# Recurrent scores built in seven halving levels, and prompt attention on queries reversed within each tile

## The reference, cut to what matters

```
# recurrence, per head: S_t = diag(f_t) S_{t-1} + k_t v_t^T ; o_t = S_t^T q_t, written in chunks
decay = exp(where(causal, G[t] - G[s], NEG))          # G: running sum of log f, per channel d
attn  = einsum("bhtd,bhtsd,bhsd->bhts", q, decay, k)  # scores inside a chunk
o     = attn @ v + einsum("bhtd,bhdv->bhtv", q * exp(G), S)
S     = exp(g_end) * S + einsum("bhsd,bhsv->bhdv", k * exp(g_end - G), v)

# prompt attention: three parts with one relative bias by distance, then a gated sum
s = einsum("btgrd,bngd->bgrtn", q, k) + rel_bias[bucket(t - n)]   # selected, window, compressed keys
p = softmax(where(valid, s, NEG)) ; o = p @ v
o_c = g[0] * o_cmp + g[1] * o_sel + g[2] * o_win
```

## Time and profile before

| what | us |
|---|---|
| median of 3 runs (3782.72 to 3790.37) | 3783.14 |
| the profiled execution, its time | 3777.45 |
| its span, first to last instruction | 3775.9 |
| recurrence, 429.2 to 1092.7 | 663.5 |
| attention rows, 1092.7 to 1171.5 | 78.8 |
| prompt attention, 1908.6 to 2346.0 | 437.4 |
| trunk, from 2657.1 | 1118.8 |

### The profile page before, as it was taken

How to read it: one execution, slowest core, us unless ns; L and a number is a source line. 1 busy time by engine, 2 the same in 40 slices (tenths; PEclk the granted TensorE clock), 3 DMA queues, 4 the chain that set the end, 5 groups by cost and what they waited for, 6 DMA issues and landing times. The chain is left out here.

```text
span 3775.9 us, 50148 instructions
## 1 busy us (share of the span) xinstructions
PE 3189.6 (84%) x19173; PEld 2945.0 (78%) x19173; DVE 1425.3 (38%) x3099; ACT 816.0 (22%) x1469; POOL 336.7 (9%) x484
## 2 busy tenths in 40 slices
PE   7999799999942788888569997447799799999999
PEld 6999798998941677677457776334699699999999
DVE  4122234234243454555335554862444422112221
ACT  3100101011000333333134454100322222111110
POOL 0011111111101222221000000000000200000000
PEclk9999878788865899999678999556899899999999
DMA  3222202112136554443121111102533111221122
GB/s 127 86 83 79 80 31 88 63 60 88 35 121 209 133 135 118 115 127 97 36 71 40 40 40 37 11 5 71 188 110 122 40 44 44 91 92 40 44 83 90
DMA packets 123489, 303.51 MB, mean 80 GB/s; under 512 B 36434, under 2 KB 60721, under 8 KB 121889
## 3 DMA queue, kind: packets, MB, share of 16 engines
q1 hardware_dynamic: 96250, 232.21, 20.6%
q0 software_dynamic: 15776, 56.93, 3.9%
q10 hardware_dynamic: 11280, 11.89, 1.0%
HBM read 233.49 MB, written 71.03 MB: 81 GB/s over the span
## 5 line engine op out<-in xcount | busy, mean ns | idle before, releaser
L2252 PE MATMUL tr_ps<-tr_act_in_r,tr_w_hi 128*128 128x364 f32 (+1 forms) x2496 | 487.3, 331 | 0.0
L2252 PEld LDWEIGHTS tr_ps<-tr_act_in_r,tr_w_hi 128*128 128x128 f32 x2496 | 428.8, 190 | 0.0
L2252 PE MATMUL tr_ps<-tr_wide_r,tr_w_hi 128*128 128x364 f32 (+1 forms) x1632 | 317.7, 330 | 0.0
L2252 PE MATMUL tr_ps<-tr_act_in_r,tr_w_r 128*128 128x364 f32 (+1 forms) x1248 | 278.8, 332 | 29.9 <-POOL tr_act_in_r L2233 22.5
L2252 PEld LDWEIGHTS tr_ps<-tr_wide_r,tr_w_hi 128*128 128x128 f32 x1632 | 279.2, 189 | 0.0
L54 PE MATMUL hg_ps<-tokens_hi,hg_gw_r 128*128 128x364 f32 (+1 forms) x576 | 224.3, 389 | 28.7 <-POOL hg_gw_r L1472 19.8
L2252 PEld LDWEIGHTS tr_ps<-tr_act_in_r,tr_w_r 128*128 128x128 f32 x1248 | 218.3, 190 | 32.9 <-issue 24.7
L2403 DVE TENSOR_TENSOR tr_w_r<-tr_w,tr_w_hi 128x1024 fp32r<-128x1024 f32 (+2 forms) x76 | 103.7, 1365 | 338.8 <-ACT tr_w_hi L2325 338.8
L55 PE MATMUL hg_ps<-tokens_r,hg_gw_hi 128*128 128x364 f32 (+1 forms) x576 | 217.9, 378 | 0.0
L56 PE MATMUL hg_ps<-tokens_hi,hg_gw_hi 128*128 128x364 f32 (+1 forms) x576 | 216.3, 376 | 0.0
L2252 PE MATMUL tr_ps<-tr_wide_r,tr_w_r 128*128 128x364 f32 (+1 forms) x816 | 181.1, 330 | 10.9 <-DVE tr_w_r L2403 10.9
(11 more groups left out here) (541 smaller groups left out, 6116.7 us busy)
## 6 DMA issues: line engine op xcount, KB each, us to landing
sa_pages<-cache_in SPq DMA_DIRECT2D x256, 256.0 KB, 3.9
tr_w<-w_gate_up_in SPq DMA_DIRECT2D x44, 512.0 KB, 3.6
proj_feat<-hg_g_stage POOLq DMA_DIRECT2D x24, 544.0 KB
tr_act_in<-proj_feat SPq DMA_DIRECT2D x24, 544.0 KB, 5.1
hg_gw<-w_gates_in SPq DMA_DIRECT2D x24, 512.0 KB
tr_w<-w_down_in SPq DMA_DIRECT2D x16, 704.0 KB, 4.1
np_wt<-w_tok_in SPq DMA_DIRECT2D x6, 1552.0 KB, 7.1
proj_tok<-np_stage_t POOLq DMA_DIRECT2D x48, 194.0 KB, 2.2
```

Of the source, the lines that this page charges most:

```text
L2252: last = pe.matmul(ps[:, 3 * bs + c, 0:z - a], wp, xp[:, k, a:z], start=(k == 0 and n == 0), stop=(k == len(tiles) - 1 and n == 2))
```

## The change

**Recurrence.** The two loops over `j` and `i` give way to seven levels `l` = 0..6. Within a tile, pairs of neighbouring halves of width 2^l meet: the queries of the later half (64 columns of each tile) are multiplied by all 128 keys, and a mask `pair` keeps the products of the earlier half of the same pair. After a level VectorE multiplies the earlier half's keys, and the later half's queries, by the other half's total decay, in place, so that keys are decayed to the end of a block twice as wide and queries to its beginning. The plain product of keys and queries (`diag_mm`) gives the diagonal. TensorE does the diagonal and each level for 8 prompt tiles, and for the sample tile in levels 0 to 2 only. Gate pieces are distributed anew: one behind the diagonal, one behind each level, and one (index 16) behind the outputs, ahead of the sum of squares. The sample's scores are multiplied by its values in one product instead of eight. The clearing of `kb` and `kt` goes; a 229 KB constant `pair` takes the place of a 64 KB one.

**Attention.** Prompt queries are reversed within each tile by a product with `flip` instead of a transpose; the bias table is then used as the DMA writes it, in two buffers, and the products and copies at each head's start go. The branch gates are turned by one product at the stage's start, ahead of their exponential, and the trunk turns the output rows back by a product with `flip`.

```
 # attention_rows_stage
+            sp.dma_start(flip[:], flip_in).then_inc(const_in, 16)
-                    pe.transpose(ps[...], rows[0:tn, t % 2, slot:slot + 2]..., ident[0:tn, 0:tn]).then_inc(tr_done, 1)
+                    if n < 4 and t0 < TP:
+                        pe.matmul(dst, src, flip[:], start=True, stop=True).then_inc(tr_done, 1)
+                    else:
+                        pe.transpose(dst, src, ident[0:tn, 0:tn]).then_inc(tr_done, 1)
 # prompt_attention_stage
+            pe.matmul(ps[:, 7, 0:NT * 3 * NH], flip[:], gates_in[:]..., start=True, stop=True).then_inc(S["gates_mm"], 1)
             for h in range(NH):
                 pe.wait_ge(head_in[h % 2], 64 * (h // 2 + 1))
-                for n in range(NTB):
-                    a, z = n * BANK, min((n + 1) * BANK, TW)
-                    if h >= 1:
-                        pe.wait_ge(S["sel_neg"], NT * h)
-                        pe.wait_ge(S["win_neg"], NT * h)
-                    pe.matmul(ps[:, n, 0:z - a], flip[:], strip[:, h % 2, a:z], start=True, stop=True)
-                pe.matmul(ps[:, NTB - 1, FAR:FAR + P], flip[:], strip_w[:, h % 2], start=True, stop=True).then_inc(S["flip_mm"], 1)
-                pe.wait_ge(S["table_set"], h + 1)
 # VectorE, per head
-                dve.wait_ge(S["flip_mm"], h + 1)
-                for n in range(NTB):
-                    a, z = n * BANK, min((n + 1) * BANK, TW)
-                    dve.tensor_copy(table[:, a:z], ps[:, n, 0:z - a])
-                dve.tensor_copy(far_w[:], ps[:, NTB - 1, FAR:FAR + P])
-                dve.drain().then_inc(S["table_set"], 1)
 # hgrn_stage, TensorE (the loops over j and i go)
+                pe.wait_ge(S["kq_set"], h + 1)
+                for t, (t0, tn) in enumerate(TILES):
+                    last = pe.matmul(ps[...], k[:, t0:t0 + tn], q[:, t0:t0 + tn], start=True, stop=True)
+                last.then_inc(S["diag_mm"], 1)
+                gate_pieces(h, AT_START, AT_START + 1)
+                for l in range(NLEV):
+                    pe.wait_ge(S["level_set"], h * (NLEV + 1) + (l + 1))
+                    if l >= 2:
+                        pe.wait_ge(S["scores_taken"], h * (NLEV + 1) + l)
+                    for t, (t0, tn) in enumerate(TILES):
...
+                        last = pe.matmul(dst..., k[:, t0:t0 + tn], halves(q_dec[:, t0:t0 + tn], l)[:, :, 1], start=True, stop=True)
+                    last.then_inc(S["level_mm"], 1)
+                    if l + 1 < NLEV:
+                        gate_pieces(h, AT_START + l + 1, AT_START + l + 2)
+                gate_pieces(h, AT_START + NLEV, AT_START + NLEV + 1)
...
                 last.then_inc(S["o_mm"], 1)
+                gate_pieces(h, AT_START + 11, 3 * CHUNKS - 1)
                 pe.wait_ge(S["sq_done"], h * 3 + 3)
                 pe.wait_ge(S["o_copied"], h + 2)
 # hgrn_stage, VectorE, per head (the memsets and both loops go)
+                dve.tensor_tensor(q_dec[:], q[:], f[:], ALU.mult).then_inc(S["level_set"], 1)
...
+                for l in range(NLEV):
+                    dve.wait_ge(S["level_mm"], h * NLEV + (l + 1))
+                    end = T if l < SLEV else TP
+                    late = halves(totals[l][:, 0:end >> l], 0)[:, :, :, 0]
+                    dve.tensor_tensor(totals[l + 1][:], late[:, :, 0], late[:, :, 1], ALU.mult)
+                    for x, t in ((0, k), (1, q_dec)):
+                        half = halves(t[:, 0:end], l)[:, :, x]
+                        dve.tensor_tensor(half, half, late[:, :, 1 - x:2 - x].to_broadcast(...), ALU.mult)
+                    dve.drain().then_inc(S["level_set"], 1)
+                    met = part[:, l % 2]
+                    dve.tensor_tensor(met, ps[:, 2 + l % 2, :]..., pair[:, l:l + 1].to_broadcast(...), ALU.mult).then_inc(S["scores_taken"], 1)
+                    dve.drain()
+                    a = halves(attn[:, 0:NTL]..., l)[:, :, 1]
+                    dve.tensor_tensor(a, a, met..., ALU.add)
 # trunk_stage
-                    last = pe.transpose(ps[...], rows[:, t, k * P:(k + 1) * P], ident[:])
+                    last = pe.matmul(ps[...], rows[:, t, k * P:(k + 1) * P], flip[:], start=True, stop=True)
```

More of the change, by code:

```diff
@@ L1387, in hgrn_stage @@
         sig = sb("sig", [P, 2, T])
-        decay = sb("decay", [P, T])
         q_dec = sb("q_dec", [P, T])
-        q_tile = sb("q_tile", [P, TP])
-        before = sb("before", [P, NTL, NBK + 1])
-        kb = sb("kb", [P, 2, T])
-        kt = sb("kt", [P, 2, TP])
+        totals = [f] + [sb(f"total{l}", [P, (T if l <= SLEV else TP) >> l]) for l in range(1, NLEV + 1)]
+        part = sb("part", [P, 2, NTL, HALF])
+        part_s = ctx.enter_context(nc.sbuf_tensor("hg_part_s", [SB * ST, SLEV, SB * ST // 2], F32))
         attn = sb("attn", [P, NTL + 1, P])
@@ L1563, in _ @@
-                for i in range(1, NBK):
-                    pe.wait_ge(S["kt_set"], h * NBK + i)
-                    for t in range(NTL):
-                        last = pe.matmul(ps[:, 3 + t // 4, (t % 4) * P + i * HC:(t % 4) * P + (i + 1) * HC], kt[:, i % 2, t * P:(t + 1) * P],
-                                         q_dec[:, t * P + i * HC:t * P + (i + 1) * HC], start=True, stop=True)
-                    last.then_inc(S["off_mm"], 1)
-                    if i % 3 == 0:
-                        gate_pieces(h, AT_START + 3 + i // 3, AT_START + 4 + i // 3)
@@ new lines, in _ @@
+                gate_pieces(h, AT_START + NLEV, AT_START + NLEV + 1)
+                pe.wait_ge(S["level_set"], h * (NLEV + 1) + (NLEV + 1))
+                for t in range(NTL):
+                    last = pe.transpose(ps[:, t // 4, (t % 4) * P:(t % 4 + 1) * P], k[:, t * P:(t + 1) * P], ident[:])
+                    if t % 4 == 3:
+                        last.then_inc(S["tr"], 1)
+                pe.transpose(ps[0:SROWS, 4, 0:P], k[:, TP:T], ident[:]).then_inc(S["tr"], 1)
+                gate_pieces(h, AT_START + 8, AT_START + 9)
@@ L1605, in _ @@
                 for n, (a, z) in enumerate(COLS):
-                    last = pe.matmul(ps[:, (3, 4, 2)[n], 0:z - a], ones[:], rstd[:, a:z], start=True, stop=True)
+                    last = pe.matmul(ps[:, 2 + n, 0:z - a], ones[:], rstd[:, a:z], start=True, stop=True)
                 last.then_inc(S["ssq_mm"], 1)
@@ L1626, in _ @@
             dve.drain()
-            f8, k8, q8, d8, qd8 = blocks(f[:]), blocks(k[:]), blocks(q[:]), blocks(decay[:]), blocks(q_dec[:])
             with dve.Fori(0, NHG) as h:
@@ L1674, in _ @@
-                dve.tensor_tensor(attn[0:SB * ST, NTL, 0:SB * ST], ps[0:SB * ST, 2, 0:SB * ST], diag[0:SB * ST, 0:SB * ST], ALU.mult)
-                dve.drain()
-                for n in range(2):
-                    a = attn[:, 4 * n:4 * n + 4, HC:P]
-                    dve.tensor_tensor(a, a, ps[:, 3 + n, :].rearrange("p (t s) -> p t s", s=P)[:, :, HC:P], ALU.add)
-                dve.memset(states[:, 0], 0.0)
+                    last = dve.tensor_tensor(attn[:, 4 * n:4 * n + 4], ps[:, n, :].rearrange("p (t s) -> p t s", s=P), ident[:].unsqueeze(1).to_broadcast([P, 4, P]), ALU.mult)
@@ L2259, in _ @@
                 for k in range(4):
-                    last = pe.transpose(ps[:, 6 + t % 2, k * P:(k + 1) * P], rows[:, t, k * P:(k + 1) * P], ident[:])
+                    last = pe.matmul(ps[:, 6 + t % 2, k * P:(k + 1) * P], rows[:, t, k * P:(k + 1) * P], flip[:], start=True, stop=True)
                 last.then_inc(tr, 1)
@@ L2577, in shape_constants @@
     p = np.arange(P)
+    pair = np.stack([((p[:, None] >> l + 1 == q >> l + 1) & (p[:, None] >> l & 1 == 0)).astype(f4) for l in range(NLEV) for q in [p[(p >> l & 1) == 1]]], axis=1)
     return {
```

187 lines of the change are left out of this document (81 added, 106 removed).

## The result

The changed kernel takes 3503.4 us in the median of 4 runs (3486.0 to 3508.2); the kernel before, timed beside it, took 3782.9. The ratio is 0.9238, with an interval from 0.9207 to 0.9269.

What follows compares the result with a forecast made beforehand. TensorE's instructions and clock were taken to bound the recurrence; in prompt attention, engines took turns at head starts. Recurrence -195, prompt attention -60, attention rows +7.5, trunk +4 sum to -243.5 us: forecast 3538 us, range 3500 to 3570.

Steps and rivals of the forecast that it cites:

- the clock gave back: Recurrence: less time at 1.2 GHz behind sparse groups, 17.5 us a head gained; rival of levels keeping low clock, chance 0.13.
- 28, 3 and 3: Recurrence, us saved a head: 28 from 248 fewer instructions, 3 from the sample's outputs, 3 from the wait ahead of line 1606.
- the hold of VectorE: Recurrence levels: GpSimd holds VectorE 2.4 us against 1.8 spare; 2.5 us a head lost, between 0 and 10.
- 3.5 us of low clock: Recurrence, loss expected to stay a head: 1.8 us behind the sample outputs and as much at the loop's end.
- The cover: Recurrence: the gate piece behind each level hides VectorE's 2.2 us update; without it, 7 x 4 x 2.2 = 62 us.
- half as long and four times as dense: Recurrence: a level, 2.0 us of 64 columns, compared with a step of line 1557; no clock loss expected behind levels.
- The seven boundaries: Prompt attention: 6.37 us from first product to first score goes at seven head starts, 44.6 us saved.
- The first scores: Prompt attention's start: scores wait for split queries and begin at 1936.2 in place of 1941.10, 4.9 us earlier.
- the clock term: Prompt attention: faster clock returns between nothing and 57 us; 10 taken.
- Neither rival: Prompt attention: all low-clock stretches go, 57 us back, 3491 (chance 0.07); or 1.2 GHz at every head's start, 3578 (0.05).
- Attention rows, +8.3 for +7.5: Attention rows: four more instructions a tile, 0.9 us each of eight tiles, plus 0.4 for one more DMA: +7.5 us.
- The step that failed: Trunk: two tiles need about 3.5 us of TensorE against a 2.53 period, so TensorE sets it: +4 us, between 0 and 6.

Runs made afterwards that it cites:

- the square: Changed kernel and three variants: levels 2 to 6 at 8 columns, 3502.7 us; all levels' products issued twice, 3551.5 us; levels 2 to 6 with both, 3561.6 us.
- the filling: Changed kernel plus one unread 320-column product behind the transposes of the first two tiles of prompt attention's heads 1 to 7 (also "the filled starts"): 3479.8 us.

## Why the prediction was right, and where its terms were off

**Recurrence, -224 for -195.** The mechanism held: TensorE set the pace with its instructions and its clock. The terms that were off, in a middle head's 55.4 us against 49: the clock gave back about 21.4 in place of 17.5 (what is left of 55.4 less 28, 3 and 3), and the hold of VectorE cost 0 in place of 2.5. Most of this clock can be seen on instructions that did not change. The gate products are the same 1,728 in both kernels; a third of them, before (after, they stand above):

```profile
L54 PE MATMUL hg_ps<-tokens_hi,hg_gw_r 128*128 128x364 f32 (+1 forms) x576 | 224.3, 389 | 28.7 <-POOL hg_gw_r L1472 19.8 <-ACT hg_g_stage L1501 8.9
```

One took 389 ns before and takes 342 now; all of them, with overlaps counted once, kept TensorE busy for 368.1 us and now for 307.6, which is 15.1 a head. The sum of squares gives 1.8 a head more. The rest lay in instructions that are gone. The wait for the first weights grew by 0.4 us (19.8 to 20.2), where I had put 1 for the larger constant.

I had left 3.5 us of low clock; a stretch of 3.4 us at half clock, 1.7 us, is what stayed. The half behind the sample outputs did not stay, because the gate piece that took the wait's place also took the low clock (852 against 477 ns with the piece moved back; in the run with the first copy ahead of the sigmoids, 3.4 us of it do lie there). That coupling was missing: I priced the wait and the clock behind it as two things. The holds occur (1.42 us for a total of 272 elements), but I set their 2.4 us against a spare of 1.8, while only the rest of GpSimd's operation is waited for. Four heads of 55.4 are 221.6 of the 224.1.

**The cover** was right in kind, not in size: 93 us in place of 62. The wait alone was smaller (46.7); the clock of uncovered levels (41.8) was not in the sum.

**Why the levels keep the clock** is shown only as far as the square goes. Of the prediction's two reasons, half as long and four times as dense, one is enough: either alone keeps 0.96 or more for the stage, and only without both does it fall to 0.90.

**Prompt attention, -55 for -60.** The seven boundaries gave 7 x 6.4 = 44.8, as forecast (44.6). The first scores came 3.2 us earlier, not 4.9: behind the gates' product (1.01 us) ScalarE now loads its table for the exponential, 1.28 us. Before, it did so at the stage's start, during the wait for the gates. The load before, then after:

```profile
1908.63 1.28 ACT L1224 ACT_TABLE_LOAD   x1 [3.79 <-PEq L75]
```

```profile
1706.00 1.28 ACT L1220 ACT_TABLE_LOAD   x1 [23.48 <-PE pa_ps L1142]
```

I had counted the instructions ahead of the exponential and not what ScalarE does when it comes to it. The rest, 7.3 us, is the clock term, of which I took 10 between 0 and 57. That it came near is luck. Counted from its first scores to those of its last tile, a head takes 34.5 us at full clock. Heads 1 to 7 took 26.7 us more than that in sum before and 15.9 after, but head 0 went from 36.6 to 39.9; in the other profile of the old code the 26.7 were 36.7, and in those of the new code without the filling the 15.9 are 4 to 16, most often 4.0 us for each head with a stretch at 1.2 GHz. Neither rival came true: in the changed kernel four heads of seven have such a stretch and three do not. What the removed wait did by itself is not shown, since the dense products went with it; that the small tiles bring the low clock without it is shown by the four heads and by the filled starts, which took it away.

**Attention rows, +8.3 for +7.5,** is shown by taking it back: 7.9 us with transposes. **Trunk, +4.1 for +4,** was right by accident. The step that failed is that the stage pays for a longer turning, TensorE setting the period there: with the same products seven of ten profiles (1118.2 to 1119.0) show no loss against the 1118.8 before. Why three show 2 to 4 us stays open.

**The rest:** the unchanged sample attention was 7.0 us shorter in this run; it took 649.5 to 662.4 in the other ones. In sum the forecast erred by 29 us in the recurrence and by 7 of chance here, both to the same side, and prompt attention took 5 of it back.

## What to carry to other kernels

An interleaved piece of dense work paid twice here, for the wait it covers and for the clock of what stands around it; price both, and price them together. When ScalarE's first exponential is made to wait for something new, count the table load that may then start only behind that wait. Before a stage's difference of one per cent is given to an edit, look at the same stage in runs whose code it did not touch.

## What the runs showed of the hardware that was not expected

- TensorE's clock fell with no idle time at all: 4 us of 8-column products and the gate piece behind them ran at 0.68, against 1.00 for the same count of 64 columns; over the stage 0.90 against 0.97.
- One unread product of 320 columns in each of two tiles was enough to hold a head at 1.00 (40.32 us against 44.36). Ahead of the first head, 20 us of busy TensorE before a 4 us wait bought nothing (0.51 behind it), while 8 us of products right up to the first scores did, in one profile (0.91 for head 0, against 0.73).
- A transpose against the reversed identity took one instruction where the product took two, 4 in place of 8 a tile in the attention rows, with 7.9 us less in the stage.
- The same attention code took 372.7 and 384.7 us in two profiles: two and four stretches of 10.2 us at 1.2 GHz, 4.0 us each, and 3.4 us in head 0 (42.4 and 45.8).
